# Loading an attention's first head inside the stage before it, and handing a convolution step and a store to other engines

## The reference, cut to what matters

```
a, q, k, v = split(h @ w_in)
u = a[..., :512] * sigmoid(a[..., 512:])
u = depthwise_conv(u, conv_w, conv_b)          # 31 taps
q, k = rope_2d(q), rope_2d(k)                  # sequence tokens only
p = softmax(q1 @ k1 * scale) - lam * softmax(q2 @ k2 * scale)
o = p @ v
```

## Time and profile before

| what | value |
| --- | --- |
| median of 3 runs | 3562.64 us (3559.93 to 3566.0) |
| the profiled execution's own time | 3563.79 us |
| span of the profiled execution | 3562.0 us |
| mean granted TensorE clock | 0.965 |
| busy share of the span | PE 93%, DVE 51%, ACT 33%, POOL 8% |

### The profile page before, as it was taken

How to read it: one execution, slowest core, us unless ns; L and a number is a source line. 1 busy time by engine, 2 the same in 40 slices (tenths; PEclk the granted TensorE clock), 3 DMA queues, 4 the chain that set the end, 5 groups by cost and what they waited for, 6 DMA issues and landing times. The chain is left out here.

```text
span 3562.0 us, 47600 instructions
## 1 busy us (share of the span) xinstructions
PE 3319.1 (93%) x18956; PEld 2779.3 (78%) x18956; DVE 1814.5 (51%) x2090; ACT 1177.3 (33%) x1915; POOL 294.2 (8%) x527
## 2 busy tenths in 40 slices
PE   7999598798999999999978898999999899999997
PEld 5887477587888888888767677888887788888886
DVE  4899467354434444444542334555555444444446
ACT  4111356364111111121155324555553321121121
POOL 0000000122000000000022111111111200000001
PEclk8999799799999999999989899999999999999999
DMA  6232866322111111111142743322212311111113
GB/s 198 66 110 82 258 200 257 115 95 72 54 36 35 41 39 38 35 35 47 49 134 83 286 140 88 104 58 53 53 41 89 84 48 59 35 47 59 35 47 118
DMA packets 277450, 313.66 MB, mean 88 GB/s; under 512 B 84841, under 2 KB 223689, under 8 KB 276273
## 3 DMA queue, kind: packets, MB, share of 16 engines
q1 hardware_dynamic: 264528, 264.46, 24.9%
q0 software_dynamic: 12768, 47.08, 3.5%
HBM read 240.93 MB, written 70.57 MB: 87 GB/s over the span
## 5 line engine op out<-in xcount | busy, mean ns | idle before, releaser
L1284 DVE TENSOR_TENSOR y_sum<-ffn_down_ps,y_sum 128x512 f32<-128x512 f32 x396 | 271.2, 690 | 236.5 <-PE ffn_down_ps L90 235.8
L88 PE MATMUL ffn_gate_ps<-y_hi,ring_hi 128*128 128x512 f32 (+1 forms) x880 | 325.7, 370 | 6.9 <-DVEq L1234 6.9
L88 PE MATMUL ffn_down_ps<-ring_hi,ffn_act_hi 128*128 128x512 f32 x792 | 312.9, 395 | 16.9 <-DVE y_sum L1284 10.4
L89 PE MATMUL ffn_gate_ps<-y_lo,ring_hi 128*128 128x512 f32 (+1 forms) x880 | 325.2, 370 | 0.0
L90 PE MATMUL ffn_gate_ps<-y_hi,ring_lo 128*128 128x512 f32 (+1 forms) x880 | 325.1, 369 | 0.0
L89 PE MATMUL ffn_val_ps<-y_lo,ring_hi 128*128 128x512 f32 (+1 forms) x880 | 323.9, 368 | 0.0
L88 PE MATMUL ffn_val_ps<-y_hi,ring_hi 128*128 128x512 f32 (+1 forms) x880 | 323.8, 368 | 0.0
L90 PE MATMUL ffn_val_ps<-y_hi,ring_lo 128*128 128x512 f32 (+1 forms) x880 | 323.7, 368 | 0.0
L89 PE MATMUL ffn_down_ps<-ring_lo,ffn_act_hi 128*128 128x512 f32 x792 | 309.7, 391 | 0.0
L90 PE MATMUL ffn_down_ps<-ring_hi,ffn_act_lo 128*128 128x512 f32 x792 | 309.3, 391 | 0.0
L1214 ACT ACTIVATE ffn_act_hi<-ffn_conv 128x1024 fp32r<-128x1024 f32 x66 | 53.4, 840 | 593.2 <-DVE ffn_conv L1264 593.2
(11 more groups left out here) (323 smaller groups left out, 6980.3 us busy)
## 6 DMA issues: line engine op xcount, KB each, us to landing
da_ada_w<-in_ada_w SPq DMA_DIRECT2D x10, 4096.0 KB, 24.4
out_raw<-in_ffn_w_up SPq DMA_DIRECT2D x44, 512.0 KB, 3.8
ffn_raw<-in_ffn_w_up SPq DMA_DIRECT2D x43, 512.0 KB, 3.8
ffn_raw<-in_ffn_w_down SPq DMA_DIRECT2D x22, 512.0 KB, 5.8
out_raw<-in_ffn_w_down SPq DMA_DIRECT2D x22, 512.0 KB, 5.6
ab_raw<-in_ab_w_in SPq DMA_DIRECT2D x20, 512.0 KB, 3.9
norm_ada<-in_ada_w SPq DMA_DIRECT2D x8, 1024.0 KB, 14.0
scratch_mla_q_hi<-up_out_hi POOLq DMA_DIRECT2D x12, 512.0 KB, 2.9
```

The lines of the kernel that those rows point to most:

```text
L88: pe.matmul(out, a_hi, b_hi, start=first, stop=False)
L89: pe.matmul(out, a_hi, b_lo, start=False, stop=False)
L1284: dve.tensor_tensor(part, down_ps[:, half, :], part, ALU.add).then_inc(s.sum_done, 1)
```

## The change

Three things are changed together.

- The queries and keys of head 0 get SBUF of their own (`FirstHead`), which outlives the projections. It shares space with the projections' `qk_hi` and weight parts `w_hi`, `w_lo`, so SP loads it inside the projections' stage when PE is through with piece 15 and all stores of queries and keys have landed. The four vectors of `lam` are loaded beside the rotation tables.
- The last convolved tile is stored by SP, not by POOL. The barrier doesn't wait for its landing; SP waits for it as the attention stage begins, ahead of its first load there.
- Step 0 of each convolution is an ACT activation (`first_step`). DVE's hand-written counts stay, over 30 steps per round. The conversion of the last value piece moves up: on ACT ahead of `copy(3, 1)`, on DVE ahead of `rotated(3, 0)`.

```diff
+class FirstHead:
+    LOADS = 6
+    def __init__(self, nc, ctx):
+        self.q, self.k_hi, self.k_lo = (ctx.enter_context(nc.sbuf_tensor(f"da_first_{n}", [P, 2, T], F32R))
+                                        for n in ("q", "k_hi", "k_lo"))
+        self.lam = ctx.enter_context(nc.sbuf_tensor("da_lam", [P, 4, B_DIM], F32))
+        self.loaded = nc.alloc_semaphore(name="first_head_in")
+        self.conv_stored = nc.alloc_semaphore(name="last_conv_stored")
+    def pieces(self, tensor):
+        return tensor[:, :, :].rearrange("p a t -> p (a t)")[:, 0:2 * KD * P]\
+            .rearrange("p (j k n) -> p j k n", j=2, n=P)
+def load_heads(sp, qk, h, q, k_hi, k_lo, signal):
+    rows = B_HEADS * 2 * B_DIM
+    def halves(part, first):
+        return qk[part][first + h * 2 * B_DIM:first + (h + 1) * 2 * B_DIM, :].rearrange("(a d) t -> d a t", a=2)
+    for part in range(2):
+        sp.dma_start(q[part * B_DIM:(part + 1) * B_DIM, :, :].bitcast(F32), halves(part, 0)).then_inc(signal, 16)
+    for k, part in ((k_hi, 0), (k_lo, 1)):
+        for copy in range(2):
+            sp.dma_start(k[copy * B_DIM:(copy + 1) * B_DIM, :, :].bitcast(F32), halves(part, rows)).then_inc(signal, 16)
...
+            sp.dma_start(head.lam[:, :, :].rearrange("p a d -> p (a d)"), row(lam_vecs.rearrange("a d -> (a d)")))\
+              .then_inc(s.tables_in.sem, 16)
             for piece in range(3, PIECES):
                 load(piece)
+            sp.wait_ge(s.full1.sem, 2 * AT * NC)
+            for stored in qk_stored:
+                sp.wait_ge(stored.sem, 32 * AT)
+            load_heads(sp, qk, 0, head.q, head.k_hi, head.k_lo, head.loaded)
+            sp.wait_ge(s.conv_done.sem, AT)
+            rows, src = conv_out[(AT - 1) * P:AT * P, :], conv[:, (AT - 1) % 2, :]
+            sp.dma_start(rows[:, 0:SEQ], src[:, 0:SEQ]).then_inc(head.conv_stored, 16)
+            sp.dma_start(rows[:, SEQ:T], src[:, SEQ + HALO:T + HALO]).then_inc(head.conv_stored, 16)
...
+            def first_step(i):
+                act.wait_ge(s.u_done.sem, (i + 1) * NC)
+                if i == 0:
+                    act.wait_ge(s.taps_in.sem, 16 * 2 * AT)
+                if i >= 2:
+                    act.wait_ge(s.conv_stored.sem, 32 * (i - 1))
+                act.activation(conv[:, i % 2, :], u[:, i % 2, 0:SPAN], ACT.Identity, scale=taps[:, i, 0:1],
+                               bias=taps[:, i, A_KERNEL:]).then_inc(s.conv_first.sem, 1)
...
                 if last:
                     v_weights(0)
+                first_step(i)
                 copy(i, 0)
                 if last:
                     v_weights(1)
                     v_weights(2)
+                    v_weights(3)
                 else:
                     weights(4 * i + 4)
                 copy(i, 1)
-                if last:
-                    v_weights(3)
...
-                    if j == 0:
-                        dve.wait_ge(s.u_done.sem, (i + 1) * NC)
-                        if i >= 2:
-                            dve.wait_ge(s.conv_stored.sem, 32 * (i - 1))
-                        dve.tensor_scalar(out, src[:, 0:SPAN], taps[:, i, 0:1], taps[:, i, A_KERNEL:],
-                                          ALU.mult, ALU.add).then_inc(s.conv_step.sem, 1)
-                        continue
-                    dve.wait_ge(s.conv_step.sem, i * (A_KERNEL - 1) + j)
+                    if j == 1:
+                        dve.wait_ge(s.conv_first.sem, i + 1)
+                    else:
+                        dve.wait_ge(s.conv_step.sem, i * (A_KERNEL - 2) + j - 1)
...
                 at = convolve(at, 3)
+                if last:
+                    v_weights(3)
                 rotated(i, 0)
                 at = convolve(at, 1)
                 rest(i, 0)
-                if last:
-                    v_weights(3)
-                else:
+                if not last:
                     weights(4 * i + 5)
...
-            store_conv(AT - 1)
-            pool.wait_ge(s.conv_stored.sem, 32 * AT)
+            pool.wait_ge(s.conv_stored.sem, 32 * (AT - 1))
...
-            head(0)
-            sp.dma_start(lam_t[:, :, :].rearrange("p a d -> p (a d)"), row(lam_vecs.rearrange("a d -> (a d)")))\
-              .then_inc(s.lam_in.sem, 16)
+            sp.wait_ge(head.conv_stored, 32)
             values(0)
             m.load(sp, 0)
-            head(1)
+            next_head(1)
...
-            dve.wait_ge(s.lam_in.sem, 16)
...
+                if n == 0 and half == 0:
+                    pe.wait_ge(head.loaded, 16 * head.LOADS)
```

More of the change, by code:

```diff
@@ L386, in turn_tensor, with __init__ @@
             mm.then_inc(s.h_turned.sem, 1)
+class FirstHead:
[18 more added lines that the diff above has]
+            sp.dma_start(k[copy * B_DIM:(copy + 1) * B_DIM, :, :].bitcast(F32), halves(part, rows)).then_inc(signal, 16)
 class FirstInputs:
-    def __init__(self, nc, ctx):
+    def __init__(self, nc, ctx, head):
         self.raw = ctx.enter_context(nc.sbuf_tensor("ab_raw", [P, 2, KD, P], F32))
-        self.w_hi, self.w_lo = (ctx.enter_context(nc.sbuf_tensor(f"ab_w_{n}", [P, 2, KD, P], F32R))
-                                for n in ("hi", "lo"))
+        self.w_hi, self.w_lo = head.pieces(head.k_hi), head.pieces(head.k_lo)
         self.work = ctx.enter_context(nc.sbuf_tensor("ab_work", [P, KD * T], F32))
@@ L608, in project_conv_diff @@
         sin_t = sb("sin", [P, SEQ])
-        qk_hi = sb("qk_hi", [P, 2, T], F32R)
+        qk_hi = head.q
         v_t = sig
@@ L1365, in __init__, with diff_attention @@
         self.turns = n - len(self.product)
-def diff_attention(nc, o_heads, qk, v_rows, lam_vecs, ident, silu, mod, ada_w, ada_b, ada_first):
+def diff_attention(nc, head, o_heads, qk, v_rows, ident, silu, mod, ada_w, ada_b, ada_first):
     KT = T // P
@@ L1424, in sb @@
             return ctx.enter_context(nc.sbuf_tensor(f"da_{label}", shape, dt))
-        q_st = sb("q_stacked", [P, 2, 2, T], F32R)
-        k_hi = sb("k_hi", [P, 2, 2, T], F32R)
-        k_lo = sb("k_lo", [P, 2, 2, T], F32R)
+        q_st = [head.q, sb("q_stacked", [P, 2, T], F32R)]
+        k_hi = [head.k_hi, sb("k_hi", [P, 2, T], F32R)]
+        k_lo = [head.k_lo, sb("k_lo", [P, 2, T], F32R)]
         v = sb("v", [P, 2, KT, P])
@@ L1433, in diff_attention @@
         o_t = sb("o", [P, 2, QP * P])
-        lam_t = sb("lam", [P, 4, B_DIM])
+        lam_t = head.lam
         lam_prod = sb("lam_prod", [P, 2, B_DIM])
@@ L1452, in _, with next_head @@
         def _(sp):
-            def head(h):
-                j, rows = h % 2, B_HEADS * 2 * B_DIM
+            def next_head(h):
                 if h >= 2:
                     sp.wait_ge(s.s2_full.sem, (h - 1) * NU)
[L1459 to L1469, removed]
+                j = h % 2
+                load_heads(sp, qk, h, q_st[j], k_hi[j], k_lo[j], qk_in[j].sem)
             def values(h):
@@ L1486, in _ @@
             m.load(sp, 2)
-            head(2)
+            next_head(2)
             m.load(sp, 3)
@@ L1490, in _ @@
             m.load(sp, 4)
-            head(3)
+            next_head(3)
             m.load(sp, 5)
@@ L1609, in scores @@
                 full, exp = ((s.s1_full, s.exp1), (s.s2_full, s.exp2))[half]
-                if n % NU == 0 and half == 0:
-                    pe.wait_ge(qk_in[j].sem, 16 * LOADS * (n // NU // 2 + 1))
+                if n == 0 and half == 0:
+                    pe.wait_ge(head.loaded, 16 * head.LOADS)
+                elif n % NU == 0 and half == 0:
+                    pe.wait_ge(qk_in[j].sem, 16 * head.LOADS * (n // NU // 2 + j))
                 if n:
                     pe.wait_ge(exp.sem, n)
-                q = q_st[:, j, half, u * P:(u + 1) * P]
+                q = q_st[j][:, half, u * P:(u + 1) * P]
                 for a, width in chunks:
@@ L1619, in scores @@
                     keys = slice(a, a + width)
-                    pe.matmul(s_ps[:, half, keys], q, k_hi[:, j, half, keys], start=True, stop=False)
-                    mm = pe.matmul(s_ps[:, half, keys], q, k_lo[:, j, half, keys], start=False, stop=True)
+                    pe.matmul(s_ps[:, half, keys], q, k_hi[j][:, half, keys], start=True, stop=False)
+                    mm = pe.matmul(s_ps[:, half, keys], q, k_lo[j][:, half, keys], start=False, stop=True)
                 mm.then_inc(full.sem, 1)
@@ L3230, in trunk @@
         silu = sb("silu", [P, KD, BLOCK])
+        heads = ExitStack()
+        head = FirstHead(nc, heads)
         with ExitStack() as layer0:
-            inputs = FirstInputs(nc, layer0)
+            inputs = FirstInputs(nc, layer0, head)
             first_norm(nc, inputs, silu, (ident, turn_a, turn_c), consts, i.c[0], i.c_ctx, i.ada_w[0, :, 0:2 * D],
@@ L3236, in trunk @@
             h_lo = layer0.enter_context(nc.sbuf_tensor("h_lo0", [P, KD, T], F32R))
-            project_conv_diff(nc, inputs, h_hi, h_lo, conv_out, qk, v_rows, i.ab_w_in[0], i.a_conv_w[0], i.a_conv_b[0],
```

(4 more changed lines are left out.)

19 lines of the change are left out of this document (9 added, 10 removed).

## The result

| | before | after |
| --- | --- | --- |
| median, in runs on one chip | 3564.32 us (3559.93 to 3568.75, 4 runs) | 3529.82 us (3527.61 to 3534.51, 4 runs) |
| profiled execution, span | 3563.79, 3562.0 us | 3527.61, 3525.8 us |
| mean granted clock | 0.965 | 0.971 |

The ratio of the times is 0.9906, with a 95% interval of 0.9894 to 0.9918: the changed kernel is about 0.9% faster, 34.5 us between the medians. 3529.0 was forecast.

A forecast was written before the change was run, and what follows sets the result against it. Three chains in turn were taken to bound it: PE in the rounds, DVE's convolution tail, then SP's and POOL's DMAs at the boundary. Saving 12.4 us there and 21.1 of loading gave 3529 us, range 3520 to 3541.

The forecast's parts named there:

- Part 1: Start of value products: last value piece ready early, removing PE's 5.24 us stall and 2.0 us of slow clock.
- Part 2: Convolution's first steps move to ACT at 1.47 us each; DVE's tail has 24 steps, its end moves 362.44 to 352.2.
- the 5.8 us: Gain on DVE from moving the first convolution steps: 6.4 us shorter tail less 0.65 for the fourth slot.
- Part 3: Last store, at the stage's end: stage ends about 353.8, next begins 3.8 us later at 357.6, 12.4 us earlier.
- Part 4: Head 0 loads before the barrier, in by 340 (350 at worst); first scores at 357.8 instead of 391.34.
- The 9.4: Time in us a value store beside head 0's loads had to land before ACT writes its buffer again.
- The sum: To PE's first scores: 33.5 us saved, 12.4 at the boundary and 21.1 of loading.
- the rivals: Late loads (0.09, 0.03), head 0 not in (0.05), value stall (0.05), ScalarE's step awaited (0.03), nothing shows (0.03).
- the stall of the value products: Rival: piece 19 lands over 5 us late, PE starts at 299.5 again, 7.5 us lost, 3537; chance 0.05.
- a later `ada_w`: Rival on the 4 MB loads in the attention: 25 us late, PE waits, 11 us lost, 3540; chance 0.09.

The follow-up runs named there:

- the run with POOL done early: Changed kernel, but SP issues the last three value stores and awaits the last two in the attention; 3527.47 us, rounds' last matmul to first scores 60.09 us.
- Head 0 alone: Changed kernel keeping only the early loads of head 0 and `lam`; first steps, last value piece and last store as before; 3544.36 us.
- the rest alone: Changed kernel, but head 0 is loaded behind the barrier, at the beginning of the attention; 3551.32 us.

## Why the prediction was right

**Part 1** held as worked out: no gap, the clock at 1.00 behind it. Undone, it costs 7.38 us (5.24 + 2.0 forecast).

**Part 2** held in its terms: 1.47 us for ACT's step, 24 steps in the tail, DVE's end at 351.30 (352.2 forecast; 0.5 of the difference is that the rounds ended earlier in this execution). What failed is what the 5.8 us were said to bring: taken by itself the edit moves DVE's end by 5.7 but the stage's end by 1.9, since in the changed kernel POOL's path ends last. The rule of the Trainium skill (ScalarE: Activation LUTs, Rules for kernel authors) that a multiply or an add belongs on VectorE agrees with the cost per step (1.47 against 0.95). It does not decide the edit: undoing it made the stretch longer, by 1.91 and by 5.65 us, which the times of whole executions don't show (3527.60 against 3529.82 for the change). In the rounds the step on ACT cost nothing, as worked out: they take 240.8 us with it and 240.9 before.

**Part 3** has the step that was misread: the 3.8 us "of barrier and clearing" taken "as the price of the stage's end". The number was right and its owner wrong. It was read where POOL was the last engine (366.2 to 369.99), and POOL's own DRAIN fills most of it:

```profile
L598 POOLq DRAIN  x1: 2839/2839/2839, 366.3 to 366.3; - x1
```

The prediction put it behind 353.8, between the end of SP's path (353.6) and the last value store's landing (354.0), as if either would pay it. By SP alone the next stage would have begun 1.0 to 1.4 us after its last issue. The landing, which came at 353.15, is POOL's wait, and does pay 3.8. That the two ends lay 0.4 us apart in the forecast, and that POOL's turned out the later, is luck, and by it the sum came out: 356.98 against 357.8. Had POOL's path been shorter, the sum would have been wrong by up to 3.4 us, what the run with POOL done early gains.

**Part 4** held: loads issued at 316.66 (318 forecast), in near 338 (340), scores waiting for no DMA. Of the pieces of `ada_w`, the slack shrank from 16.2 to 12.4 us for piece 0 and from 14.5 to 10.9 for piece 1 (issued at 365.83, landing 36.7 us later, wanted at 413.40), where it was said to stay. Before, SP issued piece 0 at 376.02 without waiting for head 0 to land, so now it is issued 18.6 us earlier, not 33.7, and it makes up most of the difference by landing in 17.0 us instead of 29.1. PE reads L165 at 386.80 (388 forecast).
The value stores beside head 0 took up to 10.2 us where 9.4 were allowed; one copy of ACT was late by 0.3 us, and PE was not. (The 9.4 took off the copy's 0.6 twice, since the 0.9 from PE's end to the issue holds it already; by the late copy some 9.9 were free.) On POOL's and SP's queues the Trainium skill (DMA: Bandwidth & Descriptors, Queues, rings and completion order) says that a DMA engine takes turns between queues but consumes one ring in order. The runs agree: 10.2 us at most beside the loads, up to 18.0 behind them.

**The sum**: 33.5 us forecast to the first scores, 33.85 measured from the rounds' last matmul. Head 0 alone brings 20.4 of it and the rest alone 13.1; 0.4 needs both. None of the rivals came. Two of them have been made to happen: the stall of the value products costs 7.4 us (7.5 forecast), and a later `ada_w` does become PE's wait.

What stays open is why POOL's DRAIN lengthens with its DMAs, and whether the microseconds that a shorter boundary saves outlast the attention.

## What to carry to other kernels

Where stages meet at a barrier, read for each engine when it arrives and how long after that the next stage begins: the same interval read behind another engine may be the wrong price. List each engine's DRAIN there: the last one to end lets the next stage begin. Giving the last waits and issues to the engine that leaves fastest (here SP), and awaiting a store where its data is next used, made the boundary 1.6 to 3.4 us shorter here, though not the whole kernel measurably faster. An edit that shortens one path is worth only what the next path leaves it, so test it with that path removed as well (1.9 us became 5.65).

## What was not expected of the hardware

- The next stage began 3.6 to 4.0 us after POOL's last wait or issue, and 1.0 to 1.4 us after SP's last issue where POOL had been done before. The difference is POOL's DRAIN: 2.10 to 3.43 us in this stage, some 0.08 us for each DMA that POOL had issued in it, against 0.12 to 0.14 for SP where SP's was the last to end.
- A pause of PE of 3.64 us ahead of the scores, in one run, left the first matmul at 0.47 us, pauses of 5.48 us and more at 0.76 to 0.80. After 6.84 us of waiting the 64 products of L165 took 6.24 us instead of 3.66.
- In one part of the attention the granted clock was 1.00 in one profile of the changed kernel and 0.88 in another, with nothing changed; by the next stage the two were 1.8 us apart, 1.6 of it from that part.
